# Rounding and subtracting each weight unit in two halves of 1024 columns

## The chip, the core and the metric

The kernel runs on one core of a Trainium2 chip. The metric is the device time of one execution in microseconds (us); lower is better. A core has TensorE (PE, matrix products; its loads of stationary operands are shown as PEld), VectorE (DVE), ScalarE (ACT), GpSimd (POOL) and SyncE (SP), which here issues the weight loads. The engines run their own instruction streams and meet at semaphores.

## What is computed

One step of a two-layer streaming encoder on 256 prompt rows and 64 sample rows of width 1024, in float32. The parts that carry most of the work:

```python
def _swiglu(h, w1, w3, w2):
    return (jax.nn.silu(h @ w1) * (h @ w3)) @ w2

# layer 0: pooling mixer, then x = x + _swiglu(h, w1_dense, w3_dense, w2_dense)
# then one K/V projection; layer 1: windowed attention, then the experts:
def _moe(h, w_router, b_router, w1, w3, w2):
    logits = h @ w_router + b_router
    vals, idx = lax.top_k(logits, TOP_K)               # 2 of 8
    gates = jax.nn.softmax(vals, axis=-1)              # spread over 8 columns: gate_full
    y = jnp.zeros_like(h)
    for e in range(N_EXPERTS):
        y = y + gate_full[..., e:e + 1] * _swiglu(h, w1[e], w3[e], w2[e])
    return y
```

Each layer ends with a gated per-layer embedding; norms stand between the parts. D_FF is 3584.

## The kernel before

**Three products for one.** TensorE multiplies float32r operands, which hold a rounded value. To keep float32 accuracy, every operand is split in a high part (the value rounded) and a low part (the value minus its high part), and each product is taken as high x high + high x low + low x high, three matmuls into the same PSUM bank.

**Weight units.** All weights come in units of 128 partitions x 2048 float32 columns (1 MB): 63 of the trunk and 42 for each of the 8 experts. SyncE loads unit q into buffer q % 6 of `raw` and signals `raw_loaded`; it waits for `lo_ready` of unit q - 6 first. ScalarE rounds the unit into `Sh` (buffer q % 3) in `hi` (line 364); before that it waits until TensorE is done with unit q - 3 (`unit_done`), whose buffer it overwrites. VectorE subtracts into `Sl` in `lo` (line 958), waits for `hi_ready` before it and signals `lo_ready`. GpSimd does this subtraction for four early units (line 314). TensorE waits for `lo_ready` in `unit` and then takes 12 wide matmuls (512 columns) for an expert's unit.

**The order is written out by hand**, for each engine in its own block, and an engine takes its instructions in that order. In the expert loop (`for n in range(NU)`, NU = 42) ScalarE and VectorE do, at step n, what the step itself needs and then `hi` or `lo` of unit n + 3. The steps follow `SEQ`: blocks of gate (g), up (u) and down (d) units, two units each. What stands between the units matters here:

- ScalarE: SiLU of a gate product (line 586), the high part of a transposed product (`high_t`, line 580), the high part of gathered rows (`high_x`, line 568), and at the expert's end the scaled results (line 598).
- VectorE: the gated product (line 1260), the low parts `low_t` and `low_x` (both through line 962), the scaled low results (line 1275), a copy of slot data (line 1226), and in steps 1 to 8 one x sum each (`add_back`, line 1241).
- TensorE: in steps 1 to 8 one scatter of the last expert's result, two narrow matmuls whose second and later ones wait for the x sum before; and the down units of the last block wait for `low_t(6)`, which stands in VectorE's order behind `lo` of unit 41.

Of the kernel before, what the change touches and what calls it, by code (L numbers as in the profile page):

```python
# [16 lines left out]
F32 = mybir.dt.float32  # L17
# [4 lines left out]
ALU = mybir.AluOpType  # L22
ACT = mybir.ActivationFunctionType
# [19 lines left out]
UNIT, NRAW, NSPL = 2048, 6, 3  # L43
# [28 lines left out]
def build(nc, A):  # L72
    ctx = ExitStack()
    with ctx:
        def sb(name, shape, dt=F32):
            return ctx.enter_context(nc.sbuf_tensor("s_" + name, shape, dt))

        def sem(name):
            return ctx.enter_context(nc.semaphore(name))

        PS = ctx.enter_context(nc.psum_tensor("PS", [P, 8, 512], F32))
        raw = sb("raw", [P, NRAW, UNIT])
        Sh, Sl = sb("Sh", [P, NSPL, UNIT], F32R), sb("Sl", [P, NSPL, UNIT], F32R)
# [88 lines left out]
        hi_ready, lo_ready, unit_done = sem("hi_ready"), sem("lo_ready"), sem("unit_done")  # L172
# [103 lines left out]
        def _(pool):  # L276
# [31 lines left out]
                pool.memset(z, 0.0).then_inc(consts, 1)  # L308
            def lo(q):

                pool.wait_ge(hi_ready, q + 1)
                if q:
                    pool.wait_ge(lo_ready, q)
                nc.gpsimd.tensor_tensor(Sl[:, q % NSPL, :], raw[:, q % NRAW, :], Sh[:, q % NSPL, :].bitcast(F32),
                                        ALU.subtract).then_inc(lo_ready, 1)

            lo(0)

            pool.wait_ge(hcat_ready, 4)
            src, n = hcat, 1  # L320
            for step, dst in enumerate((sA, sB, sA, sB)):
# [3 lines left out]
                src, n = dst, 2 * n  # L325

            lo(1)
            lo(2)

            pool.wait_ge(hcat_ready, 16)  # L330
# [21 lines left out]
        def _(act):  # L352
# [6 lines left out]
            def hi(q, r=0):  # L359

                act.wait_ge(raw_loaded[q % NRAW], r * 16 + 16 * (q // NRAW + 1))
                if q >= NSPL:
                    act.wait_ge(unit_done, r * NRAW + (q - NSPL + 1))
                nc.scalar.activation(Sh[:, q % NSPL, :], raw[:, q % NRAW, :], ACT.Copy).then_inc(hi_ready, 1)  # L364

            tables = [0]

# [23 lines left out]
            for c in range(KC):  # L391
                if c % 4 == 0:
                    act.wait_ge(x_loaded[c // 4], 16)
                nc.scalar.activation(sq3[:, c, :], xT[:, c, :], ACT.Square).then_inc(sq_ready, 1)
            hi(0)
            root(0)
            hi(1)
            hi(2)
            act.wait_ge(vec_loaded, 16)
            high_h(0)  # L400
# [158 lines left out]
            for n in range(6):  # L559
                act.wait_ge(hrow_done, n + 1)  # L560
                t, half = n // 2, n % 2
                r = TS if t == 2 else P
# [383 lines left out]
        def _(v):  # L946
# [7 lines left out]

            def lo(q, r=0):

                v.wait_ge(hi_ready, r * NRAW + (q + 1))
                nc.vector.tensor_tensor(Sl[:, q % NSPL, :], raw[:, q % NRAW, :], Sh[:, q % NSPL, :].bitcast(F32),  # L958
                                        ALU.subtract).then_inc(lo_ready, 1)

            def low(out, x, high, done):
                return nc.vector.tensor_tensor(out, x, high.bitcast(F32), ALU.subtract).then_inc(done, 1)  # L962
# [45 lines left out]
            for g, w in enumerate((2, 4, 8, 16)):  # L1008
# [15 lines left out]
                for o, a, n in ((PADP + w - 1, w - 1, TP - w + 1), (PADS, TP, TS)):  # L1024
                    last = nc.vector.scalar_tensor_tensor(out=hT[:, k, a:a + n], in0=src[:, k, o:o + n], scalar=1.0 / w, in1=hcat[:, k, o:o + n],  # L1025
                                                          op0=ALU.mult, op1=ALU.subtract)
# [13 lines left out]
            scaled(G_FFN0, 1)  # L1040
            v.wait_ge(lo_ready, 3)
            lo(3)
            v.wait_ge(pool_stored, 32)

# [6 lines left out]
            with v.Fori(0, 4) as i:  # L1051
                for j in range(6):
                    if j % 2:
                        glu_dense(i, j // 2, lambda f: G[:, bass.ds(i * (6 * T) + (j // 2 * 2 + f) * T, T)])
                    lo(Q_UP + j + NSPL, i)

            def low_gu(d, src):
                low(view(Al, GUOFF[d % 3], 2 * T), src, view(Ah, GUOFF[d % 3], 2 * T), gl_ready)

            lo(28)  # L1060
            glu_dense(0, 12, lambda f: guT[:, 24 + f, :])
            lo(29)
# [107 lines left out]
            for t in range(3):  # L1170
                last = nc.vector.max(top[:, t, :], lg[:, t, :])
            link(last)
            for t in range(3):
                last = nc.vector.max_index(topi[:, t, :], top[:, t, :], lg[:, t, :])
# [197 lines left out]
```

## Time and profile before

| | us |
|---|---|
| median of 3 runs | 1651.61 |
| lowest and highest | 1650.94, 1653.93 |
| the profiled execution | 1649.63 |
| its span | 1647.6 |

The profile is of one execution. The span runs from the first to the last instruction; the 2 us beside it lie around the program. Busy shares say how long an engine had an instruction running; a wait row says which engine's instruction ended last before a stalled one went on. The expert loop takes from about 570 to 1583 us.

### The profile page before, as it was taken

The page shows a single profiled execution, that of the slowest core. Times are in us where ns is not written, and L with a number is a line of the kernel's source. Part 1 is how long each engine was busy: PE and PEld are TensorE (multiplying, and loading weights), DVE is VectorE, ACT ScalarE, POOL GpSimd, SP SyncE. Part 2 cuts the span into 40 slices and gives each one's busy share as a digit, 9 for nine tenths or more (in the row PEclk, how much of TensorE's full clock was granted, in tenths as well). Part 3 has the DMA queues.
Part 4 walks back from the last instruction along what each step waited for, and adds up shares of the span by engine and source line. Part 5 has one row for each costly group of instructions (what it writes and reads, how often), then busy time and mean ns, then how long its engine had stood idle before and what let it go on. Part 6 is the DMA issues. An engine that isn't in the chain of part 4 may idle for free.

```text
span 1647.6 us, 22334 instructions
## 1 busy us (share of the span) xinstructions
PE 1548.9 (94%) x8088; PEld 1336.8 (81%) x8088; DVE 1202.4 (73%) x1089; ACT 975.0 (59%) x890; POOL 52.5 (3%) x45
## 2 busy tenths in 40 slices
PE   2799999998999599999999999999999999999987
PEld 1799999998989388778778778778878878878866
DVE  6643334456663388898889888888988889888874
ACT  3433333345564367767777667767767767767753
POOL 6000000010000000000000000000000000000000
PEclk7899999999999699999999999999999999999999
DMA  7154444443410389989989989989989989989920
GB/s 273 29 180 144 144 147 152 154 139 125 147 52 27 121 302 367 366 334 370 378 325 364 376 309 371 373 307 376 376 324 367 379 310 360 378 319 359 382 88 32
DMA packets 64551, 429.32 MB, mean 261 GB/s; under 512 B 8208, under 2 KB 11920, under 8 KB 13440
## 3 DMA queue, kind: packets, MB, share of 16 engines
q1 hardware_dynamic: 61232, 423.24, 68.6%
q0 software_dynamic: 1392, 4.90, 0.9%
q10 hardware_dynamic: 1888, 0.64, 0.2%
q8 instruction: 26, 0.43, 0.1%
q14 instruction: 13, 0.11, 0.0%
HBM read 425.49 MB, written 3.27 MB: 260 GB/s over the span
## 4 chain that ended last, share of the span: by engine, by line
PE 77%; DVE 9%; issue 8%; ACT 4%; DMA 1%; DVEq 0%; ACTq 0%; SPq 0%; POOLq 0%
PE PS L608 76%; ACT s_Sh L364 3%; DVE s_Al L962 2%; DVE s_Sl L958 2%; DVE s_rstd L966 1%; PE PS L899 1%; DVE s_xT L1241 1%; DVE s_hT L979 1%; DMA s_G<-rows_dram,s_ix 1%; DMA s_raw<-in_w_trunk 1%; DVE s_G L1003 1%; DVE s_hT L1025 0%; PE PS L779 0%; DVE s_G L1018 0%; DVE s_hT L1023 0%
## 5 line engine op out<-in xcount | busy, mean ns | idle before, releaser
L958 DVE TENSOR_TENSOR s_Sl<-s_raw,s_Sh 128x2048 fp32r<-128x2048 f32 x395 | 904.0, 2290 | 278.8 <-ACT s_Sh L364 277.6
L364 ACT ACTIVATE s_Sh<-s_raw 128x2048 fp32r<-128x2048 f32 x399 | 763.9, 1917 | 318.5 <-PE PS L608 314.3
L608 PE MATMUL PS<-s_Sh,s_Ah 128*128 128x512 f32 x1344 | 534.3, 398 | 15.2 <-DVE s_Al L962 15.2
L608 PE MATMUL PS<-s_Sh,s_Al 128*128 128x512 f32 x1344 | 528.1, 393 | 0.0
L608 PE MATMUL PS<-s_Sl,s_Ah 128*128 128x512 f32 x1344 | 527.3, 392 | 0.0
L608 PE MATMUL PS<-s_Ah,s_Sh 128*128 128x320 f32 x1008 | 317.5, 315 | 39.7 <-DVE s_Al L962 38.4
L608 PE MATMUL PS<-s_Al,s_Sh 128*128 128x320 f32 x1008 | 314.7, 312 | 0.0
L608 PE MATMUL PS<-s_Ah,s_Sl 128*128 128x320 f32 x1008 | 314.3, 312 | 0.0
L608 PEld LDWEIGHTS PS<-s_Sh,s_Ah 128*128 128x128 f32 x1344 | 254.7, 190 | 68.9 <-DVE s_Sl L958 19.0
L608 PEld LDWEIGHTS PS<-s_Sh,s_Al 128*128 128x128 f32 x1344 | 254.3, 189 | 55.0
L608 PEld LDWEIGHTS PS<-s_Sl,s_Ah 128*128 128x128 f32 x1344 | 254.6, 189 | 49.1
L608 PEld LDWEIGHTS PS<-s_Ah,s_Sh 128*128 128x128 f32 x1008 | 191.8, 190 | 45.8 <-issue 37.2
L608 PEld LDWEIGHTS PS<-s_Al,s_Sh 128*128 128x128 f32 x1008 | 192.1, 191 | 0.2
L608 PEld LDWEIGHTS PS<-s_Ah,s_Sl 128*128 128x128 f32 x1008 | 192.1, 191 | 0.0
L962 DVE TENSOR_TENSOR s_Al<-PS,s_Ah 128x512 fp32r<-128x512 f32 (+1 forms) x82 | 53.8, 664 | 16.0 <-ACT s_Ah L568 10.7
L586 ACT ACTIVATE s_G<-PS 128x512 f32<-128x512 f32 x56 | 33.5, 599 | 48.7 <-PE PS L608 48.7
L387 ACT ACTIVATE s_Ah<-s_hT 128x320 fp32r<-128x320 f32 x48 | 22.1, 469 | 52.7 <-DVE s_hT L1025 27.5
L411 ACT ACTIVATE s_sq<-PS 128x320 f32<-128x320 f32 x28 | 10.7, 434 | 68.4 <-PE PS L608 68.4
L341 POOL DMA_INDIRECT s_G<-rows_dram,s_ix x9 | 19.0, 2106 | 983.8 <-DVE s_ix L1222 960.9
L608 PE MATMUL PS<-s_sq,s_ones 128*128 128x320 f32 x112 | 36.6, 486 | 7.5 <-POOL s_lg L308 5.9
L415 ACT ACTIVATE s_Ah<-s_G 128x640 fp32r (+1 forms) x14 | 10.2, 736 | 53.4 <-PE PS L608 48.0
L966 DVE RECIPROCAL s_rstd<-s_std 128x320 f32<-128x320 f32 x7 | 15.1, 2153 | 35.3 <-ACT s_std L381 35.3
(156 smaller groups left out, 775.2 us busy)
## 6 DMA issues: line engine op xcount, KB each, us to landing
s_raw<-in_w_moe SPq DMA_DIRECT2D x336, 1024.0 KB, 4.8
s_raw<-in_w_trunk SPq DMA_DIRECT2D x63, 1024.0 KB, 4.9
s_xT<-in_xT SPq DMA_DIRECT2D x2, 640.0 KB, 5.1
out_yT<-s_hT SPq DMA_DIRECT2D x4, 320.0 KB, 2.4
rows_dram<-s_G SPq DMA_DIRECT2D x2, 512.0 KB, 2.8
s_pT<-in_pT ACTq DMA_DIRECT2D x1, 320.0 KB, 24.1
s_pT<-in_pT SPq DMA_DIRECT2D x1, 320.0 KB, 2.9
rows_dram<-s_G SPq DMA_DIRECT2D x1, 256.0 KB, 3.0
```

Source lines behind the costliest of these rows:

```text
L341: pool.indirect_dma_start(xrow, None, rows_dram, bass.IndirectOffsetOnAxis(ix[:, 0:1], 0)).then_inc(xrow_loaded, 16)
L364: nc.scalar.activation(Sh[:, q % NSPL, :], raw[:, q % NRAW, :], ACT.Copy).then_inc(hi_ready, 1)
L387: nc.scalar.activation(Ah3[:, c, :], hT[:, c, :], ACT.Copy).then_inc(hh_ready, 1)
L586: nc.scalar.activation(sgm[:, b % 2, :], PS[:, 2 + 2 * (b % 2), :], ACT.Silu).then_inc(msilu_done, 1)
L608: return nc.tensor.matmul(out, w, m, start=start, stop=stop, **kw)
L899: last = nc.tensor.transpose(PS[:, 0, P * q:P * q + P], gum[:, b % 2, P * q:P * q + P], ident[:, :])
L958: nc.vector.tensor_tensor(Sl[:, q % NSPL, :], raw[:, q % NRAW, :], Sh[:, q % NSPL, :].bitcast(F32), ALU.subtract).then_inc(lo_ready, 1)
L962: return nc.vector.tensor_tensor(out, x, high.bitcast(F32), ALU.subtract).then_inc(done, 1)
L966: link(nc.vector.reciprocal(rstd[:, :], std[:, :]))
L979: nc.vector.scalar_tensor_tensor(out=hT[:, c, :], in0=xT[:, c, :], scalar=vec[:, g, c:c + 1], in1=rstd[:, :], op0=ALU.mult, op1=ALU.mult). ...
L1003: nc.vector.scalar_tensor_tensor(out=hcat[:, c, o:o + b - a], in0=xT[:, c, a:b], scalar=vec[:, G_MIX0, c:c + 1], in1=rstd[:, a:b], op0=ALU ...
L1241: nc.vector.tensor_tensor(xT[:, c, :], xT[:, c, :], PS[:, bank, 0:T], ALU.add).then_inc(y_added, 1)
```

## The change

ScalarE rounds each unit by two instructions of 1024 columns, and each of them signals `hi_ready`, so this semaphore counts halves. VectorE subtracts in two instructions, each behind a wait for its own half; only the second signals `lo_ready`. GpSimd's subtractions stay whole and wait for both halves. Buffers, loads and TensorE's work are as before.

```diff
             def lo(q):
 
-                pool.wait_ge(hi_ready, q + 1)
+                pool.wait_ge(hi_ready, 2 * q + 2)
...
-                nc.scalar.activation(Sh[:, q % NSPL, :], raw[:, q % NRAW, :], ACT.Copy).then_inc(hi_ready, 1)
+                for o in (0, UNIT // 2):
+                    nc.scalar.activation(Sh[:, q % NSPL, o:o + UNIT // 2], raw[:, q % NRAW, o:o + UNIT // 2], ACT.Copy).then_inc(hi_ready, 1)
...
             def lo(q, r=0):
 
-                v.wait_ge(hi_ready, r * NRAW + (q + 1))
-                nc.vector.tensor_tensor(Sl[:, q % NSPL, :], raw[:, q % NRAW, :], Sh[:, q % NSPL, :].bitcast(F32),
-                                        ALU.subtract).then_inc(lo_ready, 1)
+                for half in range(2):
+                    v.wait_ge(hi_ready, r * (2 * NRAW) + (2 * q + half + 1))
+                    o = half * (UNIT // 2)
+                    last = nc.vector.tensor_tensor(Sl[:, q % NSPL, o:o + UNIT // 2], raw[:, q % NRAW, o:o + UNIT // 2],
+                                                   Sh[:, q % NSPL, o:o + UNIT // 2].bitcast(F32), ALU.subtract)
+                last.then_inc(lo_ready, 1)
```

VectorE near the end of an expert, from the gated product of the last block to the low part that the last down units wait for; before:

```order
L1260 TENSOR_TENSOR s_G<-s_G,PS 128x512 [waits unit_done]
L957 REGISTER_ALU
L958 TENSOR_TENSOR s_Sl<-s_raw,s_Sh 128x2048 [waits hi_ready]
L1216 ISA
L962 TENSOR_TENSOR s_Al<-PS,s_Ah 128x512 [waits xh_ready]
L1216 REGISTER_ALU
L962 TENSOR_TENSOR s_Al<-PS,s_Ah 128x512 [waits xh_ready]
L957 REGISTER_ALU
L958 TENSOR_TENSOR s_Sl<-s_raw,s_Sh 128x2048 [waits hi_ready]
L962 TENSOR_TENSOR s_Al<-PS,s_Ah 128x512 [waits th_ready]
```

and the second half of the same stretch after the change, from the second low part of gathered rows on:

```order
L966 TENSOR_TENSOR s_Al<-PS,s_Ah 128x512 [waits xh_ready]
L959 REGISTER_ALU
L961 TENSOR_TENSOR s_Sl<-s_raw,s_Sh 128x1024 [waits hi_ready]
L959 REGISTER_ALU
L961 TENSOR_TENSOR s_Sl<-s_raw,s_Sh 128x1024 [waits hi_ready]
L966 TENSOR_TENSOR s_Al<-PS,s_Ah 128x512 [waits th_ready]
```

Nothing has changed places; each unit is two instructions, and each has a register operation (the semaphore value for its wait) and a wait of its own.

ScalarE at the same place, the rounding of unit 41 and the high part behind it; before:

```order
L363 REGISTER_ALU [waits raw_loaded3]
L364 ACTIVATE s_Sh<-s_raw 128x2048 [waits unit_done]
L579 REGISTER_ALU
L580 ACTIVATE s_Ah<-PS 128x512 [waits t_done]
L363 REGISTER_ALU [waits raw_loaded4]
```

and after:

```order
L363 REGISTER_ALU [waits raw_loaded3]
L365 ACTIVATE s_Sh<-s_raw 128x1024 [waits unit_done]
L365 ACTIVATE s_Sh<-s_raw 128x1024
L580 REGISTER_ALU
L581 ACTIVATE s_Ah<-PS 128x512 [waits t_done]
L363 REGISTER_ALU [waits raw_loaded4]
```

Here the second half has neither a wait nor a register operation.

## Rows read from the trace of the kernel before

**Rows 1.** The page: busy us (share of the span); the two costliest groups.
```profile
PE 1548.9 (94%) x8088; PEld 1336.8 (81%) x8088; DVE 1202.4 (73%) x1089; ACT 975.0 (59%) x890; POOL 52.5 (3%) x45
...
L958 DVE TENSOR_TENSOR s_Sl<-s_raw,s_Sh 128x2048 fp32r<-128x2048 f32 x395 | 904.0, 2290 | 278.8 <-ACT s_Sh L364 277.6
L364 ACT ACTIVATE s_Sh<-s_raw 128x2048 fp32r<-128x2048 f32 x399 | 763.9, 1917 | 318.5 <-PE PS L608 314.3
```

**Rows 2.** Waits of the whole run: us in total, times, longest us.
```profile
DVE s_Sl L958 <- ACT s_Sh L364: 277.6, 257, 9.1
...
PE PS L608 <- DVE s_Al L962: 53.6, 21, 24.4
...
PE PS L608 <- DVE s_xT L1241: 8.5, 18, 1.8
```

**Rows 3.** Groups by form (mean ns); timeline (start, us), a plain unit.
```profile
L962 DVE TENSOR_TENSOR s_Al<-s_pT,s_Ah 128x640 fp32r<-128x640 f32 x2 | 1.6, 818 | 0.0
...
L441 ACT ACTIVATE s_Ah<-s_pT 128x640 fp32r<-128x640 f32 x1 | 0.7, 725 | 0.0
...
908.11 1.92 ACT L364 ACTIVATE s_Sh<-s_raw 128x2048 fp32r<-128x2048 f32 x1 [0.80 <-PE PS L608]
...
910.06 2.29 DVE L958 TENSOR_TENSOR s_Sl<-s_raw,s_Sh 128x2048 fp32r<-128x2048 f32 x1 [0.42 <-ACT s_Sh L364]
```

**Rows 4.** Stretches: busy PE, PEld, DVE, ACT, POOL; clock, DMA share, GB/s.
```profile
691.60:816.80 125.20, 122.66 (x562) 100.79 (x562) 110.52 (x77) 89.38 (x61) 2.23 (x1) 1.00 0.94 361
...
942.15:1069.00 126.85, 124.29 (x562) 101.93 (x563) 110.51 (x77) 89.42 (x61) 2.23 (x1) 0.99 0.92 349
...
942.00:947.00 5.00, 4.85 (x14) 3.86 (x15) 2.31 (x2) 0.51 (x2) 0.00 (x0) 0.66 0.93 275
```

**Rows 5.** Timeline, second expert's last down block: ACT, DVE, PE.
```profile
802.84 1.91 ACT L364 ACTIVATE s_Sh<-s_raw 128x2048 fp32r<-128x2048 f32 x1
...
811.89 1.92 ACT L364 ACTIVATE s_Sh<-s_raw 128x2048 fp32r<-128x2048 f32 x1 [0.73 <-PE PS L608]
813.71 0.58 ACT L580 ACTIVATE s_Ah<-PS 128x512 fp32r<-128x512 f32 x1
...
804.78 2.29 DVE L958 TENSOR_TENSOR s_Sl<-s_raw,s_Sh 128x2048 fp32r<-128x2048 f32 x1 [0.92 <-ACT s_Sh L364]
...
812.59 1.28 DVE L962 TENSOR_TENSOR s_Al<-PS,s_Ah 128x512 fp32r<-128x512 f32 x2
813.84 2.29 DVE L958 TENSOR_TENSOR s_Sl<-s_raw,s_Sh 128x2048 fp32r<-128x2048 f32 x1
816.04 0.68 DVE L962 TENSOR_TENSOR s_Al<-PS,s_Ah 128x512 fp32r<-128x512 f32 x1
...
816.86 0.49 PE L608 MATMUL PS<-s_Sh,s_Ah 128*128 128x512 f32 x1 [1.80 <-DVE s_Al L962]
```

**Rows 6.** Timeline, the second scatter of the third expert: ACT, DVE, PE.
```profile
823.80 3.72 ACT L364 ACTIVATE s_Sh<-s_raw 128x2048 fp32r<-128x2048 f32 x2
...
825.75 4.49 DVE L958 TENSOR_TENSOR s_Sl<-s_raw,s_Sh 128x2048 fp32r<-128x2048 f32 x2
830.16 0.48 DVE L1241 TENSOR_TENSOR s_xT<-s_xT,PS 128x320 f32<-128x320 f32 x1
...
830.70 0.41 PE L608 MATMUL PS<-s_PT,s_Ah 128*128 128x320 f32 x1 [0.28 <-DVE s_xT L1241]
```

**Rows 7.** Timeline, its eighth scatter: ACT, DVE, PE.
```profile
841.70 1.91 ACT L364 ACTIVATE s_Sh<-s_raw 128x2048 fp32r<-128x2048 f32 x1
...
843.63 2.29 DVE L958 TENSOR_TENSOR s_Sl<-s_raw,s_Sh 128x2048 fp32r<-128x2048 f32 x1 [0.89 <-ACT s_Sh L364]
...
849.04 0.48 DVE L1241 TENSOR_TENSOR s_xT<-s_xT,PS 128x320 f32<-128x320 f32 x1
...
846.54 0.31 PE L608 MATMUL PS<-s_PT,s_Ah 128*128 128x320 f32 x1
...
849.58 0.41 PE L608 MATMUL PS<-s_PT,s_Ah 128*128 128x320 f32 x1 [0.51 <-DVE s_xT L1241]
```

## The prediction

> **What bounds the kernel now.** I read the busy totals and the costliest groups first, then the waits, then the expert loop cut into its periods, and last the timeline around the places where TensorE stands still. TensorE is busy 94% of the span, VectorE 73%, ScalarE 59% [rows 1]. The change touches 399 rounding instructions of ScalarE and 395 subtractions of VectorE, 1917 and 2290 ns each [rows 1]; VectorE sits idle 277.6 us in front of the subtractions until ScalarE has rounded [rows 2]. That is the largest wait that the change shortens, and it is mostly not on the path: ScalarE itself waits for TensorE to give a split buffer back. In a plain stretch of the expert loop ScalarE starts on a unit at 908.11 and the next unit 2.72 us after the last, VectorE is done at 910.06 + 2.29 = 912.35 [rows 3], and TensorE needs the unit only two units, 5.4 us, after 908.11. So what counts is not the sum of waits but the places where TensorE waits for VectorE: over the run 53.6 us for low parts of activations and 8.5 us for x sums [rows 2]. Most of the 53.6 stands in the trunk, in norms that have no weight unit in their chain. In each of the eight experts there are up to three gaps: 1.80 us at the last down block [rows 5], 0.28 us at the second scatter [rows 6], 0.51 us at the eighth [rows 7]. An expert's period is 125.20 us, in four cases about 126.85 us [rows 4].
>
> **What one unit costs in two halves.** The same two operations exist on 640 columns: 725 ns on ScalarE and 818 ns on VectorE [rows 3]. On a straight line to 2048 columns, a half of 1024 columns takes 725 + 384 x (1917 - 725)/1408 = 1050 ns on ScalarE and 818 + 384 x (2290 - 818)/1408 = 1219 ns on VectorE (estimates from these rows). Back to back, instructions overlap their ends: the subtraction at 813.84 is followed at 816.04, so its pitch is 2.20 and not 2.29 us [rows 5]. Two halves then cost 2 x (1.219 - 0.08) = 2.28 us of pitch, **0.07 to 0.08 us more per unit** on VectorE, and about as much on ScalarE. The lower bound is this; the upper bound is a seam with no overlap and one handoff, 1.22 + 0.03 + 1.14 = 2.39 us, 0.19 more (0.03 is 910.06 against the end of the rounding at 908.11 + 1.92 [rows 3]). I take 0.08, since the unlinked neighbours in [rows 5] all overlap.
>
> What is gained: VectorE can start 1.05 + 0.03 us after ScalarE instead of 1.92 + 0.03. It starts 0.86 us earlier where it was waiting, and the unit is finished 0.86 - 0.08 = 0.78 us earlier. Where VectorE was not waiting, the unit only costs the 0.08.
>
> VectorE is busy 110.52 us of an expert's 125.20 [rows 4]; 42 x 0.08 = 3.4 us more fits in the 14.7 us that are free.
>
> A rule of the Trainium skill speaks against the change here. The page "VectorE: DVE Perf Modes", section on the TRN2 errata, puts a fixed 151 cycles at 0.96 GHz on every fp32 tensor_tensor and says that many small tiles pay it each. That is 157 ns for each added instruction, taken in full; for one instruction's duration the rows agree with it (2290 ns), but the pitch in [rows 5] shows half of it overlapped. By the page the gain at the first gap below would be 0.86 - 4 x 0.16 = 0.22 us instead of 0.54.
>
> **The 1.80 us gap.** TensorE starts at 816.86 as VectorE ends the low part that began at 816.04 [rows 5]. In front of it VectorE works without a pause from 804.78: four weight units with a low part, a gated product and two low x parts between them. Only the first of the four waits for ScalarE (802.84 + 1.91 = 804.75). It now starts at 802.84 + 1.05 + 0.03 = 803.92; the others have their first halves by then (the last is rounded from 811.89, first half 812.94, wanted at about 813.2). The chain moves 0.86 - 4 x 0.08 = **0.54 us** forward; 8 experts: **4.3 us**. The low part's own input comes from ScalarE at 813.71 + 0.58, 0.08 later, still ahead of 815.5.
>
> **The 0.28 us gap.** The x sum at 830.16 stands behind two units from 825.75, the first held by the rounding from 823.80 [rows 6]. It moves 0.86 - 2 x 0.08 - 0.1 (the copy of slot data in front may end that much late) = 0.6 us, more than the gap. A gap costs the stream more than it shows, because the last matmul's 0.39 us is counted while the next could have started after 0.227: for the 0.51 gap, 3.04 us lie between the scatters at 846.54 and 849.58 where nine wide matmuls (9 x 0.227) and two narrow ones (2 x 0.15) need 2.34, so 0.70, and about 0.05 more for the restart [rows 7]. So 0.28 is worth about 0.5: 7 x 0.5 = **3.5 us** (the first expert has none).
>
> **The 0.51 us gap.** The x sum at 849.04 stands behind two units; the first, at 843.63, waits for the rounding from 841.70 [rows 7]. It moves 0.86 - 0.16 = 0.70 us, about what it has to: 8 x 0.75 = **6.0 us**; with a seam of 0.18 it is 0.5 each, 4.0 in all.
>
> **The tail and the trunk.** The last expert ends in the same chain as [rows 6], there with a gap wider than the gain: another **0.6 us**. In the dense part TensorE takes much longer for a unit than in the expert loop and never waits for one, so both the gain and the seam are hidden. Only the first rounding, ahead of the first norm's root in ScalarE's queue, adds **0.1 us**. GpSimd's four subtractions stay whole and wait for two counts, which the second half gives 0.08 us later. SyncE's weight loads wait for the last half's signal, up to 0.8 us earlier than now; nothing waits for a load in the expert loop, so that buys nothing.
>
> Sum: 4.3 + 3.5 + 6.0 + 0.6 - 0.1 = 14.3 us.
>
> **The clock.** After four of the eight 1.80 us gaps TensorE's granted clock falls from 2.4 to 1.2 GHz for a few microseconds (0.66 of full speed over 942 to 947) [rows 4]; that is the 126.85 against 125.20, 1.65 us each, 6.6 in all. It never follows a gap of 0.51 or less. The new gap is 1.26 us, between the two. A straight line from none at 0.51 to half at 1.80 gives 0.29 x 8 = 2.3 of them left; that they are all gone or all stay are the ends, 0 to 6.6 us. I take about one and a half to two left, 3.5 us saved.
>
> The profiled execution took 1649.63 us, span 1647.6. The sum gives 1649.63 - 14.3 - 3.5 = 1631.8; **1631.8 us** is my forecast. The median of the three runs is 1651.61, 2 us above the profiled one, which would be one more fall of the clock; so with the clock as it is the time is 1635.3 to 1637.3.
>
> **The rivals.**
> *The gaps shrink, the clock falls as often* (chance 0.27): 1635.3 by the profile, 1637.3 by the median. For it: the 1.26 us gap stays the longest pause in an expert, behind transposes. Against it: the low clock follows only the longest gaps.
> *The seam is dear* (0.13): at 0.18 us per unit the first gap gives 0.86 - 0.72 = 0.14 us (1.1 in all), the second 0.4 (still closed or nearly, 2.8), the third 4.0, the tail 0.4: 8.3 us, 1641.3 with the clock as it is. The page's 0.16 would land here too. Against it: the overlaps in [rows 5].
> *VectorE becomes the bound, slower than before* (0.07). The second half carries a wait and, in the loop, a register operation of its own in front of it. If VectorE's sequencer did not run ahead behind a busy engine, each unit would pay a dispatch between the halves, some 0.25 us on top of 0.18. It decides from about 0.22 us, where 4 x 0.22 eats the 0.86 at the first gap, and from 14.7/42 = 0.35 VectorE is full. At 0.43 the first gap grows by 0.86 us and the expert by another 42 x 0.08 = 3.4: 8 x 4.2 = 34 us, 1684. Against it: ordinary units already have the same register operation, and still follow a low part with overlap (816.04 after 813.84 in 2.20 us) [rows 5].
> *The overlap does not happen* (0.06): VectorE still starts with the second half, for instance since something else than the rounding holds the first of each chain. Then seam and nothing else, 4 x 0.08 x 8 = 2.6 us plus small change: 1649 to 1653. Against it: the 0.03 us handoffs behind the rounding.
>
> **Chances.** My case (gaps as worked out, most falls of the clock gone) 0.47, 1627 to 1634; the others as given. A difference of 0.2%, 3.3 us, is about what can be told from none. All faster cases end below 1648: faster 0.87, the same 0.06, slower 0.07. The range must reach over the first two and half of the third: 1627 (no fall left, all gaps at their best, 1628.6, and a little) to 1641.
>
> **What would show it.** Per-instruction means of 1.05 and 1.22 us; the seam as the pitch of a pair in a full queue, 2.28 us. The gap at the last down block at about 1.26 us, the 0.28 and 0.51 us ones gone, periods near 123.4 us, and fewer with 1.65 us more. VectorE's idle time until ScalarE falls by roughly 0.86 us for each unit that waited. The forecast is wrong if the pair's pitch is above 2.4 us, if the first gap has not shrunk (then another instruction than the unit at 804.78 held the chain), or if new waits for the high halves appear in the middle of an expert.

## The result and the profile after

| | before | after |
|---|---|---|
| median, us (4 runs each, same chip) | 1652.3 | 1625.5 |
| lowest and highest | 1650.94, 1653.93 | 1624.35, 1625.96 |
| the profiled execution | 1649.63 | 1625.96 |
| its span | 1647.6 | 1623.9 |

The ratio is 0.9836, with a 95% interval of 0.9819 to 0.9853: the change makes the kernel 26.8 us faster by the medians, where 17.8 were forecast from the profiled execution; between the two profiled executions the difference is 23.7 us. The time lies 1.5 us below the low end of the range. The 39 later executions of before that stand beside the experiments have a median of 1650.69 us, 25.2 us above 1625.5. The 17 of them with a mean granted clock of 0.973 or 0.974 took 1649.04 to 1650.04 us, the 22 with 0.970 to 0.972 took 1650.48 to 1653.20.

The page of after, busy times and the two costliest groups, against [rows 1]:

```profile
PE 1535.5 (95%) x8088; PEld 1333.8 (82%) x8088; DVE 1227.1 (76%) x1484; ACT 1010.6 (62%) x1289; POOL 43.9 (3%) x45
...
L961 DVE TENSOR_TENSOR s_Sl<-s_raw,s_Sh 128x1024 fp32r<-128x1024 f32 x790 | 929.9, 1220 | 205.9 <-ACT s_Sh L365 201.4
L365 ACT ACTIVATE s_Sh<-s_raw 128x1024 fp32r<-128x1024 f32 x798 | 800.2, 1053 | 272.6 <-PE PS L609 269.2
```

and its waits (total us, times, longest), against [rows 2]:

```profile
DVE s_Sl L961 <- ACT s_Sh L365: 201.4, 155, 9.1
...
PE PS L609 <- DVE s_Al L966: 49.9, 19, 24.8
```

Halves last 1220 and 1053 ns. VectorE waits for ScalarE 76 us less, and the kernel gains about a third of that, since most of these waits cost nothing. The row of [rows 2] in which TensorE waited 8.5 us for x sums has lost its gaps inside the loop.

The second and the third expert, as stretches from one gap at the last down block to the next, against the 125.20 and 126.85 us of [rows 4]:

```profile
691.63:814.80 123.17, 122.07 (x562) 101.05 (x562) 112.99 (x119) 93.17 (x103) 1.16 (x1) 1.00 0.93 359
814.80:938.04 123.24, 122.13 (x562) 101.06 (x562) 113.00 (x119) 93.16 (x103) 1.16 (x1) 1.00 0.94 364
```

All seven periods are 123.2 to 123.3 us long, and none has the low clock that four periods of before had. VectorE is 2.5 us busier in an expert, 0.06 us per unit, and still has 10 us free.

The gap at the last down block, timeline of after (start, us): one row of ScalarE, four of VectorE, one of TensorE, against [rows 5]:

```profile
801.49 2.00 ACT L365 ACTIVATE s_Sh<-s_raw 128x1024 fp32r<-128x1024 f32 x2
...
802.57 2.36 DVE L961 TENSOR_TENSOR s_Sl<-s_raw,s_Sh 128x1024 fp32r<-128x1024 f32 x2 [0.85 <-ACT s_Sh L365]
804.85 0.68 DVE L966 TENSOR_TENSOR s_Al<-PS,s_Ah 128x512 fp32r<-128x512 f32 x1
...
811.78 2.35 DVE L961 TENSOR_TENSOR s_Sl<-s_raw,s_Sh 128x1024 fp32r<-128x1024 f32 x2
814.05 0.68 DVE L966 TENSOR_TENSOR s_Al<-PS,s_Ah 128x512 fp32r<-128x512 f32 x1
...
814.86 0.49 PE L609 MATMUL PS<-s_Sh,s_Ah 128*128 128x512 f32 x1 [1.16 <-DVE s_Al L966]
```

VectorE starts 802.57 - 801.49 = 1.08 us after ScalarE, where it was 1.94 (804.78 against 802.84 in [rows 5]). The pair's pitch is 814.05 - 811.78 = 2.27 us against 2.20. The whole chain from 802.57 to 814.05 + 0.68 lasts 12.16 us against 11.94 before, and the gap is 1.16 us instead of 1.80. The gaps of 0.28 and 0.51 us [rows 6, 7] are gone.

**Where the 23.7 us of span went.** The first expert starts at 570.96 us instead of 569.77: 1.2 lost. Its period shrinks by 1.2. The seven full periods take 1554.49 - 691.63 = 862.86 us against 1574.81 - 691.61 = 883.20: 20.3 gained, 7 x 1.96 = 13.7 by the gaps and 6.6 by the clock. What follows the last of these gaps is 3.4 shorter. Of those 3.4, 0.8 are the gap in the tail's chain (1.02 against 1.79). 2.2 are a stretch that I had not looked at, the 16 narrow matmuls of the norm behind it. The other 0.4 are not traced. Timeline and stretches of before (TensorE alone: length, busy, clock, DMA share, GB/s):

```profile
1590.72 6.75 PE L608 MATMUL PS<-s_sq,s_ones 128*128 128x320 f32 x16 [0.58 <-DVE s_xT L1241]
...
410.00:416.00 6.00, 5.01 (x24) 0.72 0.00 0
1590.70:1597.50 6.80, 6.78 (x18) 0.67 0.01 2
```

and of after:

```profile
1569.18 4.57 PE L609 MATMUL PS<-s_sq,s_ones 128*128 128x320 f32 x16 [0.59 <-DVE s_xT L1245]
...
410.00:416.00 6.00, 5.17 (x19) 0.50 0.00 0
1569.20:1573.80 4.60, 4.60 (x18) 1.00 0.02 4
```

At the tail the granted clock is 1.00 where it was 0.67. In the trunk, behind a norm's 4.5 us gap that ends at about 411, it is 0.50 where it was 0.72, so the same work takes 1.1 us longer; that is nearly all of the first expert's late start. It does not need the split: low_part_first, below, has the trunk of before unchanged, and its profile too shows 0.50 over 410 to 416 and starts the first expert at 571.05 us.

### The profile page after: what moved, and what is told of

Same layout as the page of the kernel before. It is cut to its first block, busy times and chain, and to the rows that moved or that the text cites. A ratio compares the mean times of both kernels' runs of the same rounds, so it can differ in the third digit from the quotient of the medians.

```text
span 1623.9 us, 23510 instructions
## 1 busy us (share of the span) xinstructions
PE 1535.5 (95%) x8088; PEld 1333.8 (82%) x8088; DVE 1227.1 (76%) x1484; ACT 1010.6 (62%) x1289; POOL 43.9 (3%) x45
## 4 chain that ended last, share of the span: by engine, by line
PE 86%; DVE 8%; issue 3%; ACT 2%; DMA 1%; SPq 0%; DVEq 0%; ACTq 0%; POOLq 0%
PE PS L609 84%; DVE s_Sl L961 2%; DVE s_Al L966 2%; PE PS L900 1%; DVE s_rstd L970 1%; ACT s_Sh L365 1%; DVE s_hT L983 1%; DMA s_G<-rows_dram,s_ix 1%; DMA s_raw<-in_w_trunk 1%; DVE s_G L1007 1%; PE PS L780 0%; DVE s_hT L1029 0%; DVE s_G L1022 0%; DVE s_hT L1027 0%; ACT s_std L382 0%
## 5 line engine op out<-in xcount | busy, mean ns | idle before, releaser
L961 DVE TENSOR_TENSOR s_Sl<-s_raw,s_Sh 128x1024 fp32r<-128x1024 f32 x790 | 929.9, 1220 | 205.9 <-ACT s_Sh L365 201.4
L365 ACT ACTIVATE s_Sh<-s_raw 128x1024 fp32r<-128x1024 f32 x798 | 800.2, 1053 | 272.6 <-PE PS L609 269.2
L966 DVE TENSOR_TENSOR s_Al<-s_G,s_Ah 128x640 fp32r<-128x640 f32 x14 | 11.5, 825 | 41.5 <-ACT s_Ah L416 41.5
L1053 DVE TENSOR_TENSOR s_G<-s_sq,PS 128x320 f32 (+1 forms) x28 | 12.4, 484 | 39.5 <-PE PS L609 39.5
```

Of the source, the lines that this page charges most:

```text
L365: nc.scalar.activation(Sh[:, q % NSPL, o:o + UNIT // 2], raw[:, q % NRAW, o:o + UNIT // 2], ACT.Copy).then_inc(hi_ready, 1)
L961: last = nc.vector.tensor_tensor(Sl[:, q % NSPL, o:o + UNIT // 2], raw[:, q % NRAW, o:o + UNIT // 2], Sh[:, q % NSPL, o:o + UNIT // 2].bit ...
L1053: nc.vector.tensor_tensor(out(f), sg[:, f, :], PS[:, 2 + f, 0:T], ALU.mult).then_inc(gu_ready, 1)
```

## The experiments

The theory: the time comes from two things, an earlier start of VectorE's chains and falls of the clock that long gaps bring. The rivals: one of the two splits would do alone; the finer grain helps everywhere and not in the chains alone; the clock has nothing to do with the gap. Before's medians beside these runs were 1650.69 us (dve_halves_only, act_halves_only, gap_given_back, low_part_first), 1650.04 (gap_half_back, after_and_low_part_first, chosen_units, chosen_and_low_part_first) and 1651.04 (chains_whole, last_chain_only); the ratios are to these runs of before.

### Only one engine in halves

VectorE in two halves, both behind the whole rounding:

```diff
-                nc.vector.tensor_tensor(Sl[:, q % NSPL, :], raw[:, q % NRAW, :], Sh[:, q % NSPL, :].bitcast(F32),
-                                        ALU.subtract).then_inc(lo_ready, 1)
+                for o in (0, UNIT // 2):
+                    last = nc.vector.tensor_tensor(Sl[:, q % NSPL, o:o + UNIT // 2], raw[:, q % NRAW, o:o + UNIT // 2],
+                                                   Sh[:, q % NSPL, o:o + UNIT // 2].bitcast(F32), ALU.subtract)
+                last.then_inc(lo_ready, 1)
```

> ScalarE rounds whole units as before; VectorE subtracts in two halves, both behind the whole unit, so there is a seam and no overlap. My theory (the gain is the earlier start of the first unit in each chain, the seam costs 0.07 us a unit): the pitch of a pair is 2.27 us against 2.20; the gap at the last down block grows from 1.80 by 4 x 0.07 to about 2.08 us, the gaps of 0.28 and 0.51 us by 0.14 to about 0.42 and 0.65; an expert's period grows by about 0.55 us and the clock falls at least as often: 1654 to 1661 us. Rival (halves help by themselves, for instance by freeing something earlier): no slower than before, 1652 or less.

Measured: 1651.58 us, ratio 1.0007 [0.9997, 1.0017]. TensorE and VectorE at the last down block:

```profile
816.48 2.35 DVE L959 TENSOR_TENSOR s_Sl<-s_raw,s_Sh 128x1024 fp32r<-128x1024 f32 x2
818.75 0.69 DVE L964 TENSOR_TENSOR s_Al<-PS,s_Ah 128x512 fp32r<-128x512 f32 x1
...
819.57 0.49 PE L608 MATMUL PS<-s_Sh,s_Ah 128*128 128x512 f32 x1 [2.02 <-DVE s_Al L964]
```

The seam alone, 818.75 - 816.48 = 2.27 against 2.20 us, widens the gap from 1.80 to 2.02 us, by four seams less the 0.05 us that the pair of low parts is shorter, and lengthens a period to 125.96 us. The time does not show it, because in this profile the clock fell once and not four times. My range of 1654 to 1661 us is missed by this: I had expected at least as many falls. By its time alone the run would fit the rival, "no slower than before"; the longer gaps and periods speak against it.

ScalarE in two halves, VectorE whole:

```diff
-                nc.scalar.activation(Sh[:, q % NSPL, :], raw[:, q % NRAW, :], ACT.Copy).then_inc(hi_ready, 1)
+                nc.scalar.activation(Sh[:, q % NSPL, 0:UNIT // 2], raw[:, q % NRAW, 0:UNIT // 2], ACT.Copy)
+                nc.scalar.activation(Sh[:, q % NSPL, UNIT // 2:UNIT], raw[:, q % NRAW, UNIT // 2:UNIT], ACT.Copy).then_inc(hi_ready, 1)
```

> ScalarE rounds in two halves, VectorE waits for both and subtracts the whole unit. My theory: the rounding is finished 0.08 us later and nothing overlaps, so each chain starts 0.08 us later: gaps 1.88, 0.36, 0.59 us, period 0.25 us longer, 1652 to 1658 us. Rival (ScalarE's work for others, the high parts behind the rounding, is what the halves change): gaps move by clearly more or less than 0.08 us.

Measured: 1651.29 us, ratio 1.0005 [0.9995, 1.0014]. The gap is 1.89 us, the others 0.28 and 0.52 to 0.57, the period 125.7, twice the growth that I had expected; there are two falls of the clock, and the time is just under my range. The unit that heads the chain, ACT and DVE:

```profile
803.77 1.05 ACT L364 ACTIVATE s_Sh<-s_raw 128x1024 fp32r<-128x1024 f32 x1
804.72 1.05 ACT L365 ACTIVATE s_Sh<-s_raw 128x1024 fp32r<-128x1024 f32 x1
805.80 2.29 DVE L959 TENSOR_TENSOR s_Sl<-s_raw,s_Sh 128x2048 fp32r<-128x2048 f32 x1 [0.91 <-ACT s_Sh L365]
```

VectorE starts 2.03 us after ScalarE instead of 1.94: 0.09 for ScalarE's seam. Neither split alone is worth anything; the whole gain is the overlap between the engines.

### The gap given back

The changed kernel, with a vector operation of 560 columns on data of its own, one per expert, in front of the low part that TensorE waits for:

```diff
+        pad = sb("pad", [P, 560])
...
+                        two = iota[:, None, 0:280].broadcast_to([P, 2, 280])
+                        nc.vector.tensor_tensor(pad[:, :].rearrange("p (a n) -> p a n", a=2), two, two, ALU.add)
```

> The changed kernel with one added VectorE instruction of 560 columns (about 0.65 us) per expert, in front of the low part that the last down units wait for. It writes a tile that nothing reads. Theory A (the clock falls because of the length of this gap): the gap is back at 1.8 us, the period 123.27 + 0.65 = 123.9 us, and about half of the gaps are again followed by a stretch at 1.2 GHz with 1.65 us more: 1625.5 + 8 x 0.65 + 4 x 1.65 = 1637 us. Theory B (the falls were a matter of where the gaps lay in time or of the other gaps of an expert): no falls, 1631 us.

Measured: 1637.96 us, ratio 0.9926 [0.9909, 0.9942]. The gap is 1.80 to 1.82 us again. Two periods, and short stretches behind two of the gaps:

```profile
816.42:941.93 125.51, 123.70 (x562) 102.23 (x563) 113.61 (x121) 93.21 (x103) 1.16 (x1) 0.99 0.92 355
941.93:1065.83 123.90, 122.08 (x562) 101.06 (x563) 113.60 (x121) 93.21 (x103) 1.16 (x1) 1.00 0.94 359
...
816.00:822.00 6.00, 5.58 (x17) 4.47 (x18) 2.56 (x3) 1.59 (x2) 0.00 (x0) 0.72 0.80 288
941.00:947.00 6.00, 5.07 (x22) 4.23 (x23) 4.00 (x5) 3.17 (x4) 0.00 (x0) 1.00 0.80 276
```

Five of seven periods are 125.5 us, two 123.9: the falls are back, at 1.6 us each. Nothing else of the changed kernel was altered, so the falls hang on this gap. The pad also moves every later gap in time; that this alone brings them the next run speaks against. The pad costs 12.5 us of median for 0.65 us of gap in eight experts (5.2 us); the rest is the clock.

With half the pad (280 columns in one plain operation):

```diff
+        pad = sb("pad", [P, 280])
...
+                        nc.vector.tensor_tensor(pad[:, :], iota[:, 0:280], iota[:, 0:280], ALU.add)
```

> The changed kernel with an added VectorE instruction of 280 columns (about 0.37 us) in front of the last low part, written to a tile that nothing reads: gap about 1.5 us, between the 1.16 us that were never followed by a clock fall and the 1.80 us that often were. 1625.5 + 8 x 0.37 = 1628.5 us with none; each fall in an expert adds 1.6 us. If the falls set in gradually with the gap: two or three, 1632 to 1634; if there is an edge between 1.5 and 1.8: none.

Measured: 1627.76 us, ratio 0.9858 [0.9842, 0.9875]. All eight gaps are 1.52 us, at moments of their own, no fall follows one, and the time is 2.3 us over the changed kernel's, near the 8 x 0.36 = 2.9 us of gap alone:

```profile
814.81:938.43 123.62, 122.09 (x562) 101.07 (x563) 113.31 (x121) 93.22 (x103) 1.16 (x1) 1.00 0.95 364
```

### The low part moved ahead of the last unit

The kernel before, unsplit, with the high and the low part of the last block one step earlier, in front of unit 41 on both engines (the same line goes from VectorE's block):

```diff
-                    if n == NU - 3:
```

> The kernel before, whole units, with the last block's high and low parts moved ahead of unit 41 in ScalarE's and VectorE's order, so that the last down units need not wait for unit 41's subtraction. My theory: the 1.80 us gap goes nearly away (0 to 0.2 us), worth 1.80 + 0.16 + 0.1 = about 2 us an expert, 16 us, and no clock falls, 6 to 10 us by the median; the 0.28 and 0.51 us gaps stay: 1652 - 16 - 8 = 1628 us, range 1624 to 1634. If the clock falls have nothing to do with this gap: 1636 us.

Measured: 1628.02 us, ratio 0.9861 [0.9844, 0.9877]. VectorE at the place of [rows 5], and a period:

```profile
810.07 2.29 DVE L957 TENSOR_TENSOR s_Sl<-s_raw,s_Sh 128x2048 fp32r<-128x2048 f32 x1
812.27 1.88 DVE L961 TENSOR_TENSOR s_Al<-PS,s_Ah 128x512 fp32r<-128x512 f32 x3
814.44 4.58 DVE L957 TENSOR_TENSOR s_Sl<-s_raw,s_Sh 128x2048 fp32r<-128x2048 f32 x2 [0.29 <-ACT s_Sh L364]
...
828.27:951.43 123.16, 122.37 (x563) 100.87 (x563) 110.55 (x77) 89.41 (x61) 2.22 (x1) 1.00 0.96 362
```

The 1.80 us gap is gone altogether and with it every fall of the clock; the gaps of 0.28 and 0.51 us stay. A period is 2.04 us shorter. So a move of two blocks of code, with no instruction added, reaches nearly the time of the change by another way, and the two need not exclude each other.

Both together, the changed kernel with the same move:

> The changed kernel with the last block's high and low parts ahead of unit 41. The 1.16 us gap goes, with about 0.16 us of overlapped end and 0.1 us of restart: 8 x 1.4 = 11 us under the changed kernel's 1625.5, so 1614 us. No gap over 0.3 us is left in the loop, so no clock falls. If the two changes fed on the same slack: 1625 or little below.

Measured: 1615.7 us, ratio 0.9786 [0.9769, 0.9802]. Two periods and a long stretch of the loop:

```profile
700.00:821.80 121.80, 121.80 (x564) 101.14 (x563) 113.06 (x120) 93.23 (x102) 1.16 (x1) 1.00 0.95 366
821.80:943.60 121.80, 121.80 (x564) 101.13 (x563) 113.04 (x120) 93.22 (x102) 1.16 (x1) 1.00 0.94 366
1000.00:1400.00 400.00, 400.00 (x1847) 332.14 (x1846) 370.69 (x393) 306.08 (x336) 4.64 (x4) 1.00 0.96 366
```

TensorE has no gap left in the loop. This is the fastest version, 34.3 us (2.1%) under the 1650.04 us of before beside it and 9.8 us under the changed kernel's median. Against the unsplit kernel with the same move, the split is worth 123.16 - 121.80 = 1.36 us per period: that is the price of the two scatter gaps, for which the prediction had 0.5 + 0.75.

### Only some units in halves

The cost of the seam could be spared where it buys nothing. A second semaphore counts first halves, and only the units handled at the listed steps of each expert are split, here those that head a chain (in the kernel before):

```diff
+        SPLIT = (5, 35, 40, 41)
...
-                    hi(Q_MOE + n + NSPL, i * RND)
+                    hi(Q_MOE + n + NSPL, i * RND, 0 if n in SPLIT else None)
...
+                    v.wait_ge(first_ready, first)
+                    nc.vector.tensor_tensor(Sl[:, q % NSPL, 0:h], raw[:, q % NRAW, 0:h], Sh[:, q % NSPL, 0:h].bitcast(F32), ALU.subtract)
+                    v.wait_ge(hi_ready, r * NRAW + (q + 1))
```

> Only four units of an expert are split, those whose subtraction stands first in a chain that TensorE waits for: steps 5, 35, 40 and 41; all others, and the trunk, are whole as before. My theory (the gain is the earlier start of the first unit, every further split unit only costs its seam): gap at the last down block 1.80 - 0.86 + 0.07 = 1.0 us, 0.16 shorter than in the changed kernel, the two others closed, no clock falls in the loop: 8 x 0.16 = 1.3 us faster than the changed kernel, 1624. Rival (the other units' halves count too, by a steady lead of VectorE over the whole expert): slower than the changed kernel, 1630 or more.

Measured: 1649.34 us, ratio 0.9985 [0.9974, 0.9996]. My expectation fell: the gap is still 1.80 us. ScalarE and VectorE in the chain:

```profile
806.47 1.92 ACT L367 ACTIVATE s_Sh<-s_raw 128x2048 fp32r<-128x2048 f32 x1 [0.21 <-PE PS L615]
...
804.86 1.23 DVE L967 TENSOR_TENSOR s_Sl<-s_raw,s_Sh 128x1024 fp32r<-128x1024 f32 x1
806.00 1.22 DVE L969 TENSOR_TENSOR s_Sl<-s_raw,s_Sh 128x1024 fp32r<-128x1024 f32 x1
807.14 0.68 DVE L977 TENSOR_TENSOR s_Al<-PS,s_Ah 128x512 fp32r<-128x512 f32 x1
808.43 2.29 DVE L973 TENSOR_TENSOR s_Sl<-s_raw,s_Sh 128x2048 fp32r<-128x2048 f32 x1 [0.60 <-ACT s_Sh L367]
```

The first unit starts early as planned, but the next one, rounded whole from 806.47, is ready only at 808.39: VectorE, early by now, waits 0.60 us for it and has lost its lead. Five of seven periods have a fall of the clock. In the prediction I said that only the first of the four units waits for ScalarE; that is so before the change, but the next one was ready hardly earlier than it was wanted.

The same four steps with the low part moved:

> Four split units per expert and the last block's parts ahead of unit 41. TensorE has no gap in the loop in either form, so the seams of the other 38 units are hidden: 1614 us, within 1.5 us of the form with all units split.

Measured: 1622.04 us, ratio 0.9819 [0.9803, 0.9836]. One gap of 0.31 to 0.33 us remains in an expert, at the eighth scatter, and the period is 122.8 us against 121.80 with all units split. The 1614 us that I expected are missed for the same reason: VectorE waits 0.51 us for the next unit of that chain, which is rounded whole.

Again in the kernel before, with whole chains split, all three or the last alone:

```diff
+        SPLIT = (0, 5, 6, 35, 36, 37, 38, 40, 41)
```

> Nine units of an expert are split: all that stand in the three chains (steps 35 to 38; 40, 41 and 0; 5 and 6), the other 33 and the trunk are whole. Theory C, formed from the run with four chosen units (there the second unit of the chain, rounded whole, took the first one's lead back, because its rounding ends only 0.13 us before VectorE wants it): with every unit of the chains split the lead goes through, the gap is 1.1 to 1.2 us, the other gaps closed, the period 123.2 to 123.4 us and the time 1624 to 1628, as with all units split. Rival (a lead over the whole expert counts): period above 124 us, 1632 or more.

```diff
+        SPLIT = (35, 36, 37, 38)
```

> Only steps 35 to 38, the chain before the last down block, are split. Theory C: that gap 1.1 to 1.2 us with no clock falls behind it, the gaps of 0.28 and 0.51 us as before: the period 125.2 - 0.65 = 124.6 us, 1649.6 - 8 x 0.65 - 6.6 = 1638 us and a little (1636 to 1641). Rival: the gap stays at 1.80.

Measured: 1628.1 us, ratio 0.986 [0.9843, 0.9876], and 1635.46 us, ratio 0.9902 [0.9886, 0.9919]. With all three chains, the gap and a period:

```profile
813.50 0.49 PE L615 MATMUL PS<-s_Sh,s_Ah 128*128 128x512 f32 x1 [1.15 <-DVE s_Al L977]
...
813.50:937.17 123.67, 122.39 (x562) 101.00 (x563) 111.12 (x86) 90.26 (x70) 2.22 (x1) 1.00 0.93 359
```

With the last chain alone:

```profile
816.05 0.49 PE L615 MATMUL PS<-s_Sh,s_Ah 128*128 128x512 f32 x1 [1.14 <-DVE s_Al L977]
829.87 0.41 PE L615 MATMUL PS<-s_PT,s_Ah 128*128 128x320 f32 x1 [0.28 <-DVE s_xT L1256]
848.73 0.42 PE L615 MATMUL PS<-s_PT,s_Ah 128*128 128x320 f32 x1 [0.49 <-DVE s_xT L1256]
...
816.05:940.66 124.61, 122.68 (x562) 100.81 (x563) 110.72 (x81) 89.80 (x65) 2.23 (x1) 1.00 0.93 357
```

Four split units per expert give the whole of the first term: the gap is 1.15 us, the period 125.20 - 124.61 = 0.6 us shorter, the other two gaps stand as before, and the clock falls nowhere. Against chosen_units it is 13.9 us with the same number of split units, only at other places. The sum is 8 x 0.6 + 6.6 of clock in the loop + 2.2 at the tail = 13.6, and 1649.63 - 13.6 = 1636.0 for a profiled 1635.84. The time is a little below the 1636 us at the low end of my range, since the range had no 2.2 us at the tail. Splitting nine units per expert gives a period of 123.67 us where I had expected 123.2 to 123.4 and all units split give 123.24 to 123.29. So sparing the seam elsewhere bought nothing. The chain lists were not complete either, as rows of chains_whole show, ACT, DVE and PE at the third scatter:

```profile
825.52 1.91 ACT L367 ACTIVATE s_Sh<-s_raw 128x2048 fp32r<-128x2048 f32 x1
...
827.47 2.29 DVE L973 TENSOR_TENSOR s_Sl<-s_raw,s_Sh 128x2048 fp32r<-128x2048 f32 x1 [0.90 <-ACT s_Sh L367]
829.67 0.48 DVE L1256 TENSOR_TENSOR s_xT<-s_xT,PS 128x320 f32<-128x320 f32 x1
...
830.21 0.41 PE L615 MATMUL PS<-s_PT,s_Ah 128*128 128x320 f32 x1
```

The unit of step 1 is whole; the x sum behind it ends at 829.67 + 0.48 = 830.15, and the third scatter starts at 830.21. That is 16.71 us after the gap at 813.50, where in after it is 831.29 - 814.86 = 16.43: 0.3 of the 0.4 us.

| kernel | median, us | gap at last down block | other gaps | period without a fall | falls in seven periods |
|---|---|---|---|---|---|
| before | 1652.3 | 1.80 | 0.28, 0.51 | 125.20 | 4 |
| dve_halves_only | 1651.6 | 2.02 | 0.33, 0.61 | 125.96 | 1 |
| act_halves_only | 1651.3 | 1.89 | 0.28, 0.52 to 0.57 | 125.70 | 2 |
| chosen_units | 1649.3 | 1.80 | 0.33 | 124.85 | 5 |
| gap_given_back | 1638.0 | 1.81 | none | 123.90 | 5 |
| last_chain_only | 1635.5 | 1.15 | 0.28, 0.49 | 124.61 | 0 |
| chains_whole | 1628.1 | 1.15 | none over 0.15 | 123.67 | 0 |
| low_part_first | 1628.0 | none | 0.28, 0.50 | 123.16 | 0 |
| gap_half_back | 1627.8 | 1.52 | none | 123.62 | 0 |
| after | 1625.5 | 1.16 | none | 123.24 | 0 |
| chosen_and_low_part_first | 1622.0 | none | 0.33 | 122.78 | 0 |
| after_and_low_part_first | 1615.7 | none | none | 121.80 | 0 |

The 1652.3 us of before are the four executions beside after; its later medians are 1.3 to 2.3 us lower.

## Why the prediction held and where it failed

**Durations and the seam: right.** 1.05 and 1.22 us were forecast for the halves, 1.053 and 1.220 measured; a pair's pitch 2.28, measured 2.27. The Trainium skill, page "VectorE: DVE Perf Modes", section on the TRN2 errata, lets many small tiles each pay the fixed cost. The rows disagree with this as a price in time, for instructions that stand in a full queue: the pitch grew by 0.07 us where that rule has 0.157, and the first gap gave 0.64 us where the rule would have left 0.22.

**The 1.80 us gap: 0.54 forecast, 0.64 measured.** Here 0.86 less four seams of 0.055 net was the truth: I rounded the seam up to 0.08, and the pair of low parts in the chain became 0.05 us shorter.

**The 0.28 and 0.51 us gaps: gone as forecast.** They were worth 1.36 us per expert and not 1.25. All gaps together shorten the period by 1.96 us against 1.79, which is 1.2 us over the seven.

**The clock: the step that failed.** The prediction drew a straight line from no falls after 0.51 us to half after 1.80; by it 2.3 falls would be left, and it took one and a half to two, 3.5 us of the 6.6. The falls did not thin out with the gap: all were gone in the changed kernel (3.1 us more), none came in eight gaps of 1.52 us, and five in eight of 1.81. The end of its own range for this term was what happened. There was no row between 0.51 and 1.80 us to hold the line up.

**The tail: 0.6 forecast, 3.4 measured.** I looked for low clock in the expert periods only. The norm behind the tail had it too, 6.75 us for 16 matmuls that take 4.57 at full clock, and it stood in the same trace. This 2.2 us was in no term and no bound, and without it the time would lie inside the range: the low end was the sum with every fall gone (1649.63 - 14.3 - 6.6 = 1628.7, with the gaps as worked out, not at their best) and 1.7 us for all the rest. Whether the split gave this clock back is open. The four profiles that hold the whole change all have the norm at full clock, of the eight others two; but last_chain_only has it at full clock with the tail's units whole, and chosen_units slow with them split.

**The trunk: 0.1 lost by forecast, 1.2 measured**, 1.1 of it by the clock behind one norm, which low_part_first shows without any split, so no run ties it to the change. The terms close the sum: 17.8 + 1.2 + 3.1 + 2.8 - 0.1 (first expert) - 1.1 = 23.7, which is the difference of the profiled executions. The medians differ by 3 us more, since before's median lies 2.7 us above its profile and after's 0.5 below. With four falls in the profile and falls that come in a part of the gaps only, I had read the 2 us then known as one more fall; now that all falls go, this goes too. The later executions of before fit this: the slower ones have the lower mean clock. The number of falls in them stays unseen, as they have no trace.

**The rivals.** The clock falling as often was given 0.27, and gap_given_back shows what it would have looked like. The dear seam is refuted by the pitch, VectorE as the bound by the 10 us it still has free in each expert (the 0.25 us of that rival were a supposition, and no run shows such a pause: the pair's pitch has none), and missing overlap by the start 1.08 us after ScalarE. The sign and the mechanism of the gaps were right; how the clock answers to them was not. Every large miss but the 1.2 us of the periods was a stretch of low clock.

## What to carry to other kernels

In this kernel the split between a producer and a consumer paid only where a third engine waited for the end of their chain, and only where every unit in the chain that was handed over late was split: the first alone gave nothing at the gap that mattered, four in a row gave 14 us more. (The Trainium skill, page "Perfetto Trace Analysis", section "Optimizing Scalar/DVE Operations", says that breaking up instructions may let work be completed sooner where these engines are not saturated but hold others up; the runs agree, with that condition.) Look first whether the awaited instruction can simply stand ahead of the long one: that was worth 22.7 us alone against its own runs of before, and 9.8 us by the medians on top of the split. And when a gap in TensorE shrinks, price the low clock behind all such gaps, the tail's and the trunk's too, with "all falls gone" as a case of its own: they went at once and not in proportion to the gap.

## What the runs showed of the hardware

- In the eight blocks of the expert loop the granted clock fell from 2.4 to 1.2 GHz only behind gaps of 1.80 us and more, and each fall cost 1.6 us: in before behind 4 of the 8 gaps of 1.80 us, in chosen_units behind 6 of 8 at 1.80, in gap_given_back behind 5 of 8 at 1.81, in act_halves_only behind 2 of 8 at 1.89, in dve_halves_only behind 1 of 8 at 2.01. None fell behind 1.52, 1.16 or less (8 gaps each per run). The share does not rise with the gap. The gaps of one run have the same length and the same work in front of them and behind them, and differ in the moment at which they come, so a length of 1.80 us is needed here and is not enough. No run varied the moment by itself; that it decides is not shown.
- The 16 matmuls of the tail's norm ran at full clock (4.6 us) in after, gap_given_back, gap_half_back, chains_whole, last_chain_only and after_and_low_part_first, and slowly (6.3 to 7.1 us) in before, dve_halves_only, act_halves_only, low_part_first, chosen_units and chosen_and_low_part_first. The tail's gap before it does not decide: it was 1.79 us in last_chain_only (full clock) and 1.02 in chosen_units (slow). With one profile of each, the cause stays open.
- Two subtractions of 1024 columns follow each other in 2.27 us where one of 2048 columns has a pitch of 2.20; a second wait and register operation between them cost nothing that could be seen.
